# An mLSTM's gate rows, its pieces of modulation weights and the output product of its neighbour attention, staged one product earlier and in three passes

## The reference

```
mod = silu(c) @ w_ada + b_ada                       # six groups of 2048: sh1, sc1, ga1, sh2, sc2, ga2
h = modulate(rms_norm(x, g_norm1), sh1, sc1)
qa, ka, va, oa, gates, qb, kb, vb = split(h @ w_in) # seven of 1024 columns, gates of 16
h_a = mlstm_bidirectional(qa, ka, va, gates)        # 4 heads of 256, forward and backward
h_a = h_a * rsqrt(mean(h_a**2) + eps) * g_head_a * sigmoid(oa)
h_b = neighborhood_attention(qb, kb, vb, rpb)       # 8 heads of 128
x = x + ga1 * (concat([h_a, h_b]) @ w_out)
x = x + ga2 * conv_glu(modulate(rms_norm(x, g_norm2), sh2, sc2), ...)
out = rms_norm(x, g_final)
```

## Time and profile before

| | |
|---|---|
| median of three timed runs | 2317.61 us (2315.53 to 2318.05) |
| the profiled execution | 2316.93 us, span 2315.1 us |
| TensorE busy | 2170.8 us (94% of the span) |
| VectorE busy | 1733.4 us (75%) |
| ScalarE busy | 953.9 us (41%) |
| chain that ended last | PE 81%, DVE 7%, DMA 5%, ACT 3%, issue 3% |
| granted TensorE clock, mean | 0.976 |
| `qa` with neighbour attention | 1150.5 to 1209 us |
| `ka`, `va`, `oa` | 1209 to 1355 us |
| `mg`, then `out2b` with the mLSTM | 1355 to 1361, 1362.75 to 1480 us |
| `out2a` | 1481 to 1533 us |

### The profile page before, as it was taken

How to read it: one execution, slowest core, us unless ns; L and a number is a source line. 1 busy time by engine, 2 the same in 40 slices (tenths; PEclk the granted TensorE clock), 3 DMA queues, 4 the chain that set the end, 5 groups by cost and what they waited for, 6 DMA issues and landing times.

```text
span 2315.1 us, 39250 instructions
## 1 busy us (share of the span) xinstructions
PE 2170.8 (94%) x15305; PEld 2043.6 (88%) x15305; DVE 1733.4 (75%) x2349; ACT 953.9 (41%) x1480; POOL 214.0 (9%) x130
## 2 busy tenths in 40 slices
PE   2389999999999999999999999899999999999997
PEld 2389997889999978999999987799999999988886
DVE  6989997797899967878858857778785666554554
ACT  2145445235444343354354422255544444343443
POOL 0000580000008500051000000000000000000000
PEclk9599999999999999999999999999999999999999
DMA  9989956795997587879949975257876555565553
GB/s 330 353 279 348 306 164 230 266 326 174 346 349 240 148 312 232 292 187 323 327 133 349 363 258 162 82 191 255 274 251 179 183 182 181 181 218 185 188 193 125
DMA packets 390350, 559.32 MB, mean 242 GB/s; under 512 B 25543, under 2 KB 316943, under 8 KB 389724
## 3 DMA queue, kind: packets, MB, share of 16 engines
q1 hardware_dynamic: 386304, 550.70, 72.1%
q0 software_dynamic: 1456, 4.28, 0.8%
q10 hardware_dynamic: 2476, 2.82, 0.4%
HBM read 555.57 MB, written 2.18 MB: 241 GB/s over the span
## 4 chain that ended last, share of the span: by engine, by line
PE 81%; DVE 7%; DMA 5%; ACT 3%; issue 3%; SPq 0%; ACTq 0%; POOL 0%; DVEq 0%; POOLq 0%
PE gemm L1626 77%; DMA w_raw<-in_w_in 2%; DMA ada_first<-in_ada_w 2%; DVE w_lo L1110 1%; PE bankO L1703 1%; DVE ada_even L1078 1%; ACT w_hi L764 1%; PE stat L1648 1%; DVE ada_odd L1078 1%; DVE ada_acc L1097 0%; PE bankS L1809 0%; PE bankS L1810 0%; DVE scr L1150 0%; PE bankO L1899 0%; PE bankT L1714 0%
## 5 line engine op out<-in xcount | busy, mean ns | idle before, releaser
L1626 PE MATMUL gemm<-h_hi,w_hi 128*128 128x256 f32 (+1 forms) x3312 | 947.5, 286 | 24.1 <-DVE h_lo L1155 19.0
L1626 PE MATMUL gemm<-h_lo,w_hi 128*128 128x256 f32 (+1 forms) x3312 | 943.2, 285 | 0.0
L1626 PE MATMUL gemm<-h_hi,w_lo 128*128 128x256 f32 (+1 forms) x3312 | 943.0, 285 | 0.0
L1110 DVE TENSOR_TENSOR w_lo<-w_raw,w_hi 128x1024 fp32r<-128x1024 f32 (+1 forms) x524 | 634.9, 1225 | 381.2 <-ACT w_hi L764 380.5
L764 ACT ACTIVATE w_hi<-w_raw 128x1024 fp32r<-128x1024 f32 (+1 forms) x588 | 604.0, 1041 | 693.9 <-PE gemm L1626 540.9
L1626 PEld LDWEIGHTS gemm<-h_hi,w_hi 128*128 128x128 f32 (+1 forms) x3312 | 638.2, 193 | 26.4 <-issue 21.6
L1626 PEld LDWEIGHTS gemm<-h_lo,w_hi 128*128 128x128 f32 (+1 forms) x3312 | 638.0, 193 | 0.6
L1626 PEld LDWEIGHTS gemm<-h_hi,w_lo 128*128 128x128 f32 (+1 forms) x3312 | 638.0, 193 | 0.3
L1078 DVE SCALAR_TENSOR_TENSOR ada_even<-ada_raw,c_act,ada_even 128x1024 f32<-128x1024 f32 x160 | 212.7, 1329 | 5.8 <-DMA ada_raw<-in_w_ada 2.5
L638 POOL TENSOR_TENSOR w_lo<-w_raw,w_hi 128x1024 fp32r<-128x1024 f32 x64 | 160.6, 2516 | 415.3 <-ACT w_hi L764 415.2
L1078 DVE SCALAR_TENSOR_TENSOR ada_odd<-ada_raw,c_act,ada_odd 128x1024 f32<-128x1024 f32 x128 | 171.8, 1342 | 5.6 <-DMA ada_raw<-in_ada_w 2.6
(11 more groups left out here) (323 smaller groups left out, 2633.0 us busy)
## 6 DMA issues: line engine op xcount, KB each, us to landing
w_raw<-in_w_in SPq DMA_DIRECT2D x264, 512.0 KB, 5.5
w_raw<-in_w_up SPq DMA_DIRECT2D x176, 512.0 KB, 3.6
ada_raw<-in_ada_w SPq DMA_DIRECT2D x160, 512.0 KB, 7.1
ada_raw<-in_w_ada SPq DMA_DIRECT2D x160, 512.0 KB, 5.0
w_raw<-in_w_out SPq DMA_DIRECT2D x96, 512.0 KB, 6.4
w_raw<-in_w_down SPq DMA_DIRECT2D x88, 512.0 KB, 3.7
ada_first<-in_ada_w SPq DMA_DIRECT2D x32, 512.0 KB, 8.8
ada_late<-in_w_ada SPq DMA_DIRECT2D x32, 512.0 KB, 5.2
```

The lines of the kernel that those rows point to most:

```text
L1110: dve.tensor_tensor(w_lo[:, fixed % PARTS, 0:sz], w_raw[:, fixed % RAW, 0:sz], w_hi[:, fixed % PARTS, 0:sz].bitcast(F32), ALU.subtract).th ...
L1626: last = pe.matmul(half(g, k, q), left, right, start=(kt == 0 and j == 0), stop=(u == len(g.units) - 1 and t == nk - 1 and j == len(parts) ...
```

## The change

- Group 9's pieces go beside `qa` and `ka`, group 10's beside `va` and `oa`; beside `out2b` there are none.
- `mg` comes right behind `qa`. The gate-row matmuls and ScalarE's part stand at step 3 of `ka`, VectorE's `gate_rows` at step 4. GpSimd makes `sel`, `g_bias` and `one_row` once attention's outputs are read.
- `ka` and `oa` are written out in one body of four blocks, without a loop.
- Beside `oa` the attention output `qbT` is split into `qb_hi` and `qb_lo` (ScalarE at steps 1 and 5, VectorE at 2 and 6), and `out2b` is done in three passes.
- The mLSTM's heads start at step 0 of `out2b`, the end of heads 2 and 3 stands at steps 12 to 15.
- Buffers are laid out anew: `hA` where `h_hi` was, `hA_hi` over `kaT`, the rows where attention's bias and logits were.

```diff
-MLSTM_FIRST = 3
+ROWS_STEP = 3
+QB_STEPS = (1, 5)
...
-        hA = at("hA", B1 + 16, [P, CT, T])
+        hA = at("hA", 80, [P, CT, T])
-        hA_hi = at("hA_hi", B1 + 52, [P, CT, T], F32R)
-        hA_lo = at("hA_lo", B1 + 16, [P, CT, T], F32R)
+        hA_hi = at("hA_hi", B1 + 24, [P, CT, T], F32R)
+        hA_lo = at("hA_lo", 80, [P, CT, T], F32R)
+        qb_hi = at("qb_hi", B1 + 16, [P, NH, T], F32R)
+        qb_lo = at("qb_lo", B1 + 8, [P, NH, T], F32R)
-        g_T = at("g_T", 111, [4 * NHA, T])
+        g_T = at("g_T", B1 + 40, [4 * NHA, T])
...
-        G["qa"] = product("qa", w2, 4, CB, full, 4, "a", h_hi, h_lo, plain(0))
-        G["ka"] = product("ka", w2, 4, CB, full, 2, "a", h_hi, h_lo, plain(O_KA), ada=(9, 0, 1))
-        G["va"] = product("va", w2, 4, CB, full, 2, "b", h_hi, h_lo, plain(O_VA), ada=(9, 16, 1))
-        G["oa"] = product("oa", w2, 4, CB, full, 2, "a", h_hi, h_lo, plain(O_OA), ada=(10, 0, 1))
+        G["qa"] = product("qa", w2, 4, CB, full, 4, "a", h_hi, h_lo, plain(0), ada=(9, 0, 1))
         G["mg"] = product("mg", w2, 1, 4 * NHA, full, 1, "s", h_hi, h_lo, plain(O_G))
-        G["out2b"] = product("out2b", a["w_out_2"][0, DC:2 * DC], 8, CB, full[0:2], 8, "a", qbT, None, plain(0),
-                             ada=(10, 16, 1))
+        G["ka"] = product("ka", w2, 4, CB, full, 4, "a", h_hi, h_lo, plain(O_KA), ada=(9, 16, 1))
+        G["va"] = product("va", w2, 4, CB, full, 2, "b", h_hi, h_lo, plain(O_VA), ada=(10, 0, 1))
+        G["oa"] = product("oa", w2, 4, CB, full, 4, "a", h_hi, h_lo, plain(O_OA), ada=(10, 16, 1))
+        G["out2b"] = product("out2b", a["w_out_2"][0, DC:2 * DC], 8, CB, full[0:2], 8, "a", qb_hi, qb_lo, plain(0))
...
-            wait_out(pool, G["mg"])
+            pool.wait_ge(o_read, NH * 3)
...
-            halves(G["ka"], lambda i, k, q: tile_of(kaT, i, k, q, 2), ACT.Copy)
+            narrow(G["mg"], g_T)
+            def gate_inputs(_, s):
+                if s != ROWS_STEP:
+                    return
+                act.wait_ge(rows_ready, 1)
+                act.wait_ge(gate_bias_loaded, 16)
+                for d in range(2):
+                    act.activation(i_row[:, d, :], bankT[0:NHA, d * T:(d + 1) * T], ACT.Identity,
+                                   bias=g_bias[:, 2 * d:2 * d + 1])
+                    ins = act.activation(f_row[:, d, :], bankS[0:NHA, d * T:(d + 1) * T], ACT.Identity,
+                                         bias=g_bias[:, 2 * d + 1:2 * d + 2])
+                link(ins)
+                link(act.activation(l_row[:], f_row[:], ACT.Abs))
+                link(act.activation(l_row[:], l_row[:], ACT.Exp, scale=-1.0))
+                act.activation(l_row[:], l_row[:], ACT.Ln, bias=1.0).then_inc(soft_ready, 1)
+            halves(G["ka"], lambda i, k, q: tile_of(kaT, i, k, q, 4), ACT.Copy, beside=gate_inputs)
             halves(G["va"], lambda i, k, q: va_tok[:, q, bass.ds(i * (2 * CB) + k * CB, CB)], ACT.Copy)
-            halves(G["oa"], lambda i, k, q: tile_of(oaT, i, k, q, 2), ACT.Sigmoid)
-            narrow(G["mg"], g_T)
+            act.wait_ge(rows_done, 1)
+            def queries_high(_, s):
+                if s in QB_STEPS:
+                    j = 4 * QB_STEPS.index(s)
+                    split_hi(qbT[:, j:j + 4, :], qb_hi[:, j:j + 4, :])
+            halves(G["oa"], lambda i, k, q: tile_of(oaT, i, k, q, 4), ACT.Sigmoid, beside=queries_high)
             def mlstm(_, s):
                 if s == 0:
-                    act.wait_ge(rows_ready, 1)
...
-                    act.activation(l_row[:], l_row[:], ACT.Ln, bias=1.0).then_inc(soft_ready, 1)
-                elif s == MLSTM_FIRST:
                     stat_wait(act, "cols")
                     act.activation(a_col[:].rearrange("p d t h -> p (d t h)"), stat[:, 0:4 * NHA], ACT.Copy).then_inc(stat_read, 1)
                     act.wait_ge(stat_read, USE["cols"] + 1)
-                h, d = divmod(s - MLSTM_FIRST, 3)
+                h, d = divmod(s, 3)
                 if 0 <= h < NHA and d < 2:
                     n = 2 * h + d
                     act.wait_ge(decay_in, n + 1)
                     for t in range(TT):
                         act.activation(decay[:, d, t, :], decay[:, d, t, :], ACT.Exp, bias=a_col[:, d, t, h:h + 1])
                     act.activation(floor_[:, d, :], bankT[:, T:2 * T], ACT.Exp, scale=-1.0).then_inc(decay_done, 1)
-                if d == 0 and h >= 1:
+                if d == 0 and 1 <= h <= NHA:
                     head_square(h - 1)
-                if d == 1 and h >= 1:
+                if d == 1 and 1 <= h <= NHA:
                     head_root(h - 1)
-                if d == 1 and h >= 2:
+                if d == 1 and 2 <= h <= NHA:
                     head_high(h - 2)
+                if s == 3 * NHA + 3:
+                    head_high(NHA - 1)
...
-            head_high(NHA - 2)
-            head_root(NHA - 1)
-            head_high(NHA - 1)
...
-            through(G["ka"])
-            through(G["va"])
-            through(G["oa"])
-            through(G["mg"])
-            mod_out(9)
...
-                if s == 1:
-                    gate_rows()
-                h, step = divmod(s - MLSTM_FIRST, 3)
+                h, step = divmod(s, 3)
...
+                    elif step == 2:
+                        head_low(NHA - 2)
+                        head_norm(NHA - 1)
+                if s == 3 * NHA + 3:
+                    head_low(NHA - 1)
...
+            through(G["mg"])
+            through(G["ka"], none, lambda _, s: gate_rows() if s == ROWS_STEP + 1 else None)
+            through(G["va"])
+            def queries_low(_, s):
+                if s - 1 in QB_STEPS:
+                    j = 4 * QB_STEPS.index(s - 1)
+                    split_lo(qbT[:, j:j + 4, :], qb_hi[:, j:j + 4, :], qb_lo[:, j:j + 4, :])
+            through(G["oa"], none, queries_low)
+            mod_out(9)
             dve.wait_ge(mask_done, 2)
-            wait_out(dve, G["mg"])
             through(G["out2b"], residual(G["out2b"], 8), mlstm)
-            head_low(NHA - 2)
-            head_norm(NHA - 1)
-            head_low(NHA - 1)
...
-            multiply(G["ka"])
+            multiply(G["mg"])
+            def gate_inputs(_, s):
+                if s != ROWS_STEP:
+                    return
+                wait_out(pe, G["mg"])
+                pe.wait_ge(o_read, NH * 3)
+                for kind, dst in enumerate((bankT, bankS)):
+                    for d in range(2):
+                        c = 2 * NHA * d + NHA * kind
+                        last = pe.matmul(dst[0:NHA, d * T:(d + 1) * T], ident[0:4 * NHA, c:c + NHA], g_T[:],
+                                         start=True, stop=True)
+                last.then_inc(rows_ready, 1)
+            multiply(G["ka"], gate_inputs)
             multiply(G["va"])
             multiply(G["oa"])
-            multiply(G["mg"])
...
-                elif s == MLSTM_FIRST:
+                h, step = divmod(s, 3)
+                if h == NHA and step == 1:
+                    head_sum(NHA - 1)
...
-            wait_out(pe, G["mg"])
-            pe.wait_ge(o_read, NH * 3)
-            multiply(G["out2b"], mlstm)
-            head_sum(NHA - 1)
-            multiply(G["out2a"], ready=(mix_ready, lambda t: 2 * LAYERS + t // 2))
+            multiply(G["out2b"], mlstm, ready=(mix_ready, lambda t: 2 * LAYERS + t // 4))
+            multiply(G["out2a"], ready=(mix_ready, lambda t: 2 * LAYERS + 2 + t // 2))
```

More of the change, by code:

```diff
@@ L205, in program @@
         hstd = at("hstd", B1 + 50, [P, 2, T])
-        hA_hi = at("hA_hi", B1 + 52, [P, CT, T], F32R)
-        hA_lo = at("hA_lo", B1 + 16, [P, CT, T], F32R)
-        g_T = at("g_T", 111, [4 * NHA, T])
[L210 to L217, removed]
+        hA_hi = at("hA_hi", B1 + 24, [P, CT, T], F32R)
[3 more added lines that the diff above has]
+        g_T = at("g_T", B1 + 40, [4 * NHA, T])
+        f_row = at("f_row", B1 + 41, [NHA, 2, T])
+        l_row = at("l_row", B1 + 43, [NHA, 2, T])
+        b_row = at("b_row", B1 + 45, [NHA, 2, T])
+        one_row = at("one_row", B1 + 47, [NHA, T])
+        g_bias = at("g_bias", B1 + 48, [NHA, 4])
+        m_row = at("m_row", B1 + 52, [NHA, 2, 2, T])
+        i_row = at("i_row", B1 + 56, [NHA, 2, T])
+        sel = at("sel", B1 + 58, [NHA, NHA, P])
         a_col = at("a_col", 96, [P, 2, TT, NHA])
@@ L986, in mlstm @@
-                    link(ins)
-                    link(act.activation(l_row[:], f_row[:], ACT.Abs))
-                    link(act.activation(l_row[:], l_row[:], ACT.Exp, scale=-1.0))
-                    act.activation(l_row[:], l_row[:], ACT.Ln, bias=1.0).then_inc(soft_ready, 1)
-                elif s == MLSTM_FIRST:
                     stat_wait(act, "cols")
@@ L1853, in mlstm @@
                 if s == 0:
-                    for kind, dst in enumerate((bankT, bankS)):
-                        for d in range(2):
-                            c = 2 * NHA * d + NHA * kind
```

(4 more changed lines are left out.)

## The result

The changed kernel took 2320.02 us in the median (2318.14 to 2322.93), the kernel before 2316.61 on the same chip: a ratio of 1.0016, with a 95% interval of 1.0010 to 1.0023. The median lies 0.7 us from the forecast of 2319.3. The change itself is +3.4 us where +1.7 was forecast; at the median that is under 0.2%, and the end of the interval reaches just over it. The profiled execution took 2320.48 us (span 2318.7; before 2315.1).

What follows compares the result with a forecast made beforehand. TensorE bounds plain products, VectorE's chain ends each `out2b` head cycle. Terms +3.8 (`qa`), +1.9 (gate rows), +2.4 (`ka`), -11.0 (`out2b`), -1.4 and +6.0 (clock) give +1.7 on 2317.61: 2319.3 us, range 2308 to 2326.

Steps and rivals of the forecast that it cites:

- The first part of `out2b`: From the first unit's start to head 0's first broadcast: 5.7 us instead of 22.16, difference -16.5.
- The order of the head's chain: In `out2b`'s heads, w_hi waits behind exponential, load and root; VectorE's chain sets the second numerator; heads +3.2 us in all.
- The clock: In `out2b`'s heads, waits of TensorE drop its clock: 2.5 falls of 2.4 us, +6.0 (between 0 and 14).
- Rival (b): Clock falls to 1.2 GHz in all four heads, 4 x 3.3 us instead of 6.0: 2326 us; chance 0.13.
- `qa`: +6.0 for +3.8: Ada pieces on VectorE's way to the maximum lengthen `qa` by 3.8 us (bounds 0 and 9.6).
- nothing behind: In `qa`, the pieces add 0.7, 0.5, 0 and 0.25 us at steps 4 to 7, and nothing after.
- `ka`: 0.43 us for +2.4: In `ka`, TensorE waits for unit 9's w_lo, late behind the gate rows: +2.4 us (bounds 0 and 5).
- (a): ScalarE hides the split in `out2b`, VectorE's chain as before, no new clock falls: 2306 us; chance 0.24 with halfway case.
- halfway case: Forecast's longer chain in `out2b`'s heads but no fall of the clock: 2313 us; within (a)'s chance of 0.24.
- (c): VectorE falls behind in `qa` with pieces in all eight steps, +9.6 instead of 3.8: 2325 us; 0.13 together with (d).
- (d): Gate rows still late or the tail before `out2a` still waits, shrinking the -16.5: 2325 us; 0.13 together with (c).
- The table switch: Before the root in `out2b`'s heads, a switch costs the load's 1.28 us, without the skill's drain of about 1.38.

Runs made afterwards that it cites:

- kernel with filler: Seven float32 matmuls per head with unread results, four ahead of the second denominator, three ahead of the second numerator, added to the changed kernel: 2312.29 us, ratio 0.9982.

## Why the prediction was right, step by step

**Confirmed in place and size.** The first part of `out2b`: 5.95 us, predicted 5.7. The order of the head's chain: the second numerators at 15.7, 17.5, 17.8 and 19.9 us behind the broadcasts, where the working gives 15.9, 17.65, 17.8 and 20.0. The tail without a long wait: 0.39 us ahead of `out2a`'s second unit, predicted 0.35. The fall of the clock ahead of `out2a` gone: -1.3, predicted -1.4.

**The clock: the right mechanism, a little too small.** I put 2.5 falls of 2.4 us, 6.0. There were four, one in each head, at 1.5 to 2.9 us each against the kernel with filler, and they cost 7.7 us in the medians and 8.2 in the rows. Rival (b) had the count right and the price (4 x 3.3) too high. Head 0, where I saw no fall, has one too.

**`qa`: +6.0 for +3.8.** The steps that I laid out by hand came as written. At the second and fourth scores TensorE waits 1.46 and 1.40 us where it waited 0.29 and 0.20, the next two 0.35 and 0.34, and up to there the step starts have moved by 3.5 us against my 3.6. At the last scores it is 3.8 us, my figure. The step that failed is "nothing behind": I followed the maximum and stopped where the scores end, and 2.2 us more came behind them. Behind the maximum VectorE also copies each attention output out of its bank, and that copy stands behind w_lo and piece:

```profile
1190.31 1.23 DVE L1122 TENSOR_TENSOR w_lo<-w_raw,w_hi 128x1024 fp32r<-128x1024 f32 x1
1191.45 1.28 DVE L1090 SCALAR_TENSOR_TENSOR ada_odd<-ada_raw,c_act,ada_odd 128x1024 f32<-128x1024 f32 x1
...
1194.89 0.42 DVE L1433 COPY qbT<-bankO 128x256 f32<-128x256 f32 x1
```

VectorE has no idle time left ahead of the first of these. TensorE's next output waited 0.63 us for that last copy, two later ones 0.58 and 0.29 us. These waits are 1.5 of the 2.2 us; the rest has no wait of its own in the rows.

**`ka`: 0.43 us for +2.4.** The chain on ScalarE was taken over from `out2b`, where it holds two table loads (kernel before: ahead of the exponential, then of the logarithm):

```profile
1371.44 1.28 ACT L988 ACT_TABLE_LOAD   x1
...
1373.38 1.28 ACT L989 ACT_TABLE_LOAD   x1
```

In `ka` of the changed kernel no load stands ahead of the exponential:

```profile
1241.60 0.47 ACT L981 ACTIVATE i_row<-bankT,g_bias 4x256 f32<-4x256 f32 x1 [0.76 <-PE bankS L1869]
...
1244.48 1.28 ACT L988 ACT_TABLE_LOAD   x1
...
1246.83 1.99 ACT L766 ACTIVATE w_hi<-w_raw 128x1024 fp32r<-128x1024 f32 x2
...
1256.57 0.39 PE L1643 MATMUL gemm<-h_hi,w_hi 128*128 128x256 f32 x1 [0.43 <-DVE w_lo L1122]
```

From the first i_row to the logarithm's end are 4.8 us instead of 6.1, and ScalarE also started 0.3 us sooner behind the matmuls. So the w_hi of unit 8 starts 7.15 us behind the gate-row matmuls' start (1239.68), predicted 8.9, and the w_lo of unit 9 ends at 16.8, predicted 18.6. TensorE was ready for it at 16.5, predicted 16.3 (18.6 less 16.3 is 2.3, not the 2.4 that went into the sum). A stall that is the difference of two long paths is only as good as the longer of them.

The errors of +2.2 in `qa`, -2.0 in `ka` and about +2 in the clock partly cancelled, and so the sum was nearer to the time than its terms: +1.7 predicted, +3.6 in the span. That the forecast of 2319.3 is only 0.7 us off is luck on top: it was added to 2317.61, the median of three runs, where twenty gave 2316.61.

**The rivals.** (a), ScalarE hides the split, fell: in head 1 VectorE stands idle for 3.38 us until the w_hi is there. Its halfway case, my chain at full clock, gave 2313; the filler made that case, and it took 2312.29. (c) had `qa` as a bound with +9.6; it was +6.0. (d) fell: the columns don't wait, and `out2a`'s second unit waits 0.39 us.

**The table switch.** The root starts 1.29 us behind the start of a load of 1.28. Leaving it out brought the chain forward by 1.4 us in each of heads 1 to 3. By the Trainium skill ("ScalarE: Activation LUTs", section "What ACT_TABLE_LOAD costs"), at 2.66 us a switch with its drain, I estimate that it would have been about twice that. The trace does not agree with it here, and the row was the right price.

## What to carry to other kernels

Putting a product into three cheaper passes moves work onto the engines that split its weights. Where one of them also carries a chain with exponential and root, ask where in its queue the split will stand, not how much idle time it has: in head 1 VectorE waited 3.38 us for a w_hi of 1.04 us, the second numerator came 2.85 us later than with the native product, and one step's difference in the order was worth 10.7 us. When a piece of work is moved into a stage, follow every product of the engine that takes it, down to the copies that empty a bank, and not just the one that closes the loop today. A change of several parts is worth taking apart even when its sum is near zero: this one held a part worth 15.8 us.

## What the runs showed of the hardware

TensorE's clock fell after waits that I had thought too short. In head 1 it stood still for 2.68 us, worked for 1.1 us and stood still for 1.32 us, and the numerator behind that ran at 1.2 GHz. In head 0, where I foresaw no fall, 2.05 and 1.32 us did the same:

```profile
1389.94 1.10 PE L1654 MATMUL stat<-wts,ones_and_halves 128*128 128x256 f32 x4 [2.05 <-DVE den L1480]
1392.36 3.78 PE L1924 MATMUL bankO<-wts,va_tok 128*128 128x256 f32 x8 [1.32 <-DVE hA L1486]
```

So did 1.93 and 1.32 us with the root left out; there the granted clock fell within the numerator, at about 1417.6 us. With 0.17 and 1.32 us in head 1 it stayed at 1.00:

```profile
1414.46 1.10 PE L1654 MATMUL stat<-wts,ones_and_halves 128*128 128x256 f32 x4 [0.17 <-DVE den L1480]
```

This is a row of the kernel with the root one step later. The Trainium skill ("TensorE: Matmul & The Clock Gate", section "A second HAM failure mode: psum-queue depth-cycling") says of a bf16 kernel that frequent brief pauses between groups of matmuls were enough to make the clock swing between its levels; these runs agree, for waits of 0.4 to 3.2 us in a chain of engines, and give it a price, 1.5 to 2.9 us for each fall. Seven matmuls a head whose result nobody reads kept the clock at 1.00 throughout.
